# Gate and up projections of a SwiGLU block: eight block products per pair of weight tiles, or seven by Strassen's scheme

## The reference, cut to what matters

```
x = x + W_out( sigmoid(gA) * windowed_attention(h) + sigmoid(gB) * gated_linear_attention(h) )   # h = rmsnorm(x)
h = rmsnorm(x, g_ffn)
x = x + (silu(h @ w_gate) * (h @ w_up)) @ w_down        # w_gate, w_up: 1024 x 2816, w_down: 2816 x 1024
```

## Time and profile before

| | us |
|---|---|
| median of 3 runs | 994.57 |
| lowest and highest run | 994.55, 995.9 |
| span of the profiled execution | 994.7 |
| TensorE busy in it | 959.4 (96%) |
| DVE, ACT, POOL busy | 469.1, 352.6, 325.3 |

### The profile page before, as it was taken

The page is one execution under the profiler, slowest core; times in us unless marked ns, Lnnn a source line. Parts: engine busy times, 40 slices in busy tenths (PEclk is TensorE's granted clock), DMA queues, the critical chain, the costliest instruction groups (busy, mean ns, idle before and its releaser), DMA issues.

```text
span 994.7 us, 17842 instructions
## 1 busy us (share of the span) xinstructions
PE 959.4 (96%) x7171; PEld 897.7 (90%) x7171; DVE 469.1 (47%) x970; ACT 352.6 (35%) x661; POOL 325.3 (33%) x139
## 2 busy tenths in 40 slices
PE   3999999999889999999999999999999999999997
PEld 3899999988878787878789999999999999999997
DVE  5673656647777557776755344222113222122321
ACT  5542433434444444344434443222112222122231
POOL 2442312122222112222323334443334444334450
PEclk9999999999999999999999999999999999999999
DMA  8332213231222211121115222223223223323212
GB/s 228 88 84 64 75 53 65 53 75 51 69 65 64 64 43 43 52 56 43 43 29 168 86 85 86 84 84 105 86 80 89 84 84 91 91 77 90 65 55 68
DMA packets 148787, 76.34 MB, mean 77 GB/s; under 512 B 19280, under 2 KB 147622, under 8 KB 148726
## 3 DMA queue, kind: packets, MB, share of 16 engines
q1 hardware_dynamic: 142582, 71.88, 25.9%
q10 hardware_dynamic: 6144, 3.61, 1.3%
HBM read 71.87 MB, written 3.60 MB: 76 GB/s over the span
## 4 chain that ended last, share of the span: by engine, by line
PE 82%; DVE 12%; ACT 3%; issue 2%; DMA 1%; SPq 0%; ACTq 0%; DVEq 0%
PE G L487 23%; PE G L489 22%; PE G L488 22%; PE X L650 3%; PE X L621 2%; DVE qAT L1315 2%; PE X L634 2%; DVE den L1354 1%; DVE rs L1118 1%; DVE rs L1117 1%; DVE rt L1119 1%; DVE rv L1280 1%; DMA xtok<-in_x_sample_dram 1%; PE X L580 1%; ACT rs L894 1%
## 5 line engine op out<-in xcount | busy, mean ns | idle before, releaser
L465 POOL TENSOR_TENSOR w_lo<-wraw,w_hi 128x1024 fp32r<-128x1024 f32 x129 | 323.6, 2508 | 645.3 <-ACT w_hi L807 645.2
L487 PE MATMUL G<-h_hi,w_hi 128*128 128x272 f32 x1280 | 382.7, 299 | 11.0 <-DVE rv L1280 8.6
L489 PE MATMUL G<-h_hi,w_lo 128*128 128x272 f32 x1280 | 371.0, 290 | 0.0
L488 PE MATMUL G<-h_lo,w_hi 128*128 128x272 f32 x1280 | 369.0, 288 | 0.0
L487 PEld LDWEIGHTS G<-h_hi,w_hi 128*128 128x128 f32 x1280 | 241.6, 189 | 30.7 <-issue 28.0
L488 PEld LDWEIGHTS G<-h_lo,w_hi 128*128 128x128 f32 x1280 | 242.0, 189 | 0.6
L489 PEld LDWEIGHTS G<-h_hi,w_lo 128*128 128x128 f32 x1280 | 241.5, 189 | 0.0
L487 PE MATMUL G<-f_hi,w_hi 128*128 128x272 f32 x704 | 203.0, 288 | 0.0
L489 PE MATMUL G<-f_hi,w_lo 128*128 128x272 f32 x704 | 202.9, 288 | 0.0
L488 PE MATMUL G<-f_lo,w_hi 128*128 128x272 f32 x704 | 202.1, 287 | 0.0
L807 ACT ACTIVATE w_hi<-wraw 128x1024 fp32r<-128x1024 f32 x129 | 135.3, 1049 | 89.1 <-PE G L489 89.1
(11 more groups left out here) (217 smaller groups left out, 968.7 us busy)
## 6 DMA issues: line engine op xcount, KB each, us to landing
wraw<-in_w_in_dram SPq DMA_DIRECT2D x45, 512.0 KB
wraw<-in_w_gate_dram SPq DMA_DIRECT2D x22, 512.0 KB
wraw<-in_w_up_dram SPq DMA_DIRECT2D x22, 512.0 KB
wraw<-in_w_down_dram SPq DMA_DIRECT2D x16, 512.0 KB
xtok<-in_x_prompt_dram SPq DMA_DIRECT2D x8, 512.0 KB, 5.2
wraw<-in_w_in_dram SPq DMA_DIRECT2D x16, 256.0 KB
wraw<-in_w_out_dram SPq DMA_DIRECT2D x8, 512.0 KB
wraw<-in_w_down_dram SPq DMA_DIRECT2D x8, 384.0 KB
```

Of the source, the lines that this page charges most:

```text
L465: pool.tensor_tensor(w_lo[:, slot, :, :], wraw[:, slot, :, :], w_hi[:, slot, :, :].bitcast(F32), ALU.subtract).then_inc(w_split, 1)
L487: pe.matmul(o, w_hi[:, slot, kc, :], b_hi[:, kc, cols], start=(kc == 0), stop=False)
L488: pe.matmul(o, w_hi[:, slot, kc, :], b_lo[:, kc, cols], start=False, stop=False)
L489: mm = pe.matmul(o, w_lo[:, slot, kc, :], b_hi[:, kc, cols], start=False, stop=(kc == last))
```

## The change

For one pair of tiles, gate (n) and up (n+1), the weights are taken as a 2 x 2 matrix of blocks: A11 and A12 are the gate tile's first and last 512 input rows, A21 and A22 the up tile's. The activations are B11, B12 (first 512 features, frame halves one and two), B21, B22. Plain multiplication takes eight block products A x B of 4 chunks each; Strassen's scheme in Winograd's form takes seven with sums of blocks:

- DVE makes of the weights A21 + A22, A21 - A11 (in place in `wraw`), A21 + A22 - A11 and A12 - (A21 + A22 - A11) (`sums`); ACT rounds three of them to `c_hi` (`sums_high_part`), POOL subtracts for two low parts and DVE for one (`sums_low_part` on each).
- DVE makes of the activations B12 - B11 (`fa`) and, for the blocks 4 to 7, five kinds of input (`fb`), once, in the output projection (`ffn_input`).
- TensorE runs seven products of 12 matmuls per pair q (`gate_up`) into four banks, BANKS[q % 2]; three of them add onto a bank that ACT or DVE has read in between (`copy_p1`, `evict_early`). DVE puts the results together (`evict_early`, `evict_late`), and the silu follows one pair later (`gated`).
- The loops of the stage are written out instead of hardware loops. The residual comes by columns into a ring of two (`xcol`) instead of as whole rows, EARLY is 2 instead of 3, and the memory plan is another.

```diff
+PAIRS = [(g, GU0[g] + 2 * i) for g, m in enumerate(FF_GROUPS) for i in range(m)]
+FIRST = [sum(FF_GROUPS[:g]) for g in range(len(FF_GROUPS))]
...
-EARLY = 3
+EARLY = 2
...
+        BANKS = [[G[1][:, 0:TH], G[1][:, 512:512 + TH], G[0][:, 0:TH], G[0][:, 512:512 + TH]],
+                 [X[0][:, 0:TH], X[0][:, 512:512 + TH], X[1][:, 0:TH], X[1][:, 512:512 + TH]]]
...
+            def weights(n, w, row0, kc, col):
+                sp.wait_ge(w_split, n - RING + 1)
+                if n - RING in PAIR_OF:
+                    sp.wait_ge(sums_ok, PAIR_OF[n - RING] + 1)
...
+            def residual(i):
+                if i >= 2:
+                    sp.wait_ge(xt_done, i - 1)
+                c = slice(i * P, (i + 1) * P)
...
+                pool.wait_ge(c_hi_ok, 2 * q + 1)
+                pool.tensor_tensor(c_lo[q % 2][:, 0:2], csum[:, 0:2], c_hi[q % 2][:, 0:2].bitcast(F32),
+                                   ALU.subtract).then_inc(c_lo_ok, 1)
+            for n in range(N_TILES):
                 pool.wait_ge(hi_done, n + 1)
                 low_part(n % RING)
+                if n in PAIR_OF and n - 1 in PAIR_OF and PAIR_OF[n] == PAIR_OF[n - 1]:
+                    sums_low_part(PAIR_OF[n])
...
+            def product(bank, a_hi, a_lo, b_hi, b_lo, adds=False, ready=None):
+                for kc in range(HK):
+                    if ready is not None:
+                        pe.wait_ge(f_ok, ready + kc + 1)
+                    pe.matmul(bank, a_hi[:, kc, :], b_hi[:, kc, :], start=(kc == 0 and not adds), stop=False,
+                              skip_group_check=adds)
+                    pe.matmul(bank, a_hi[:, kc, :], b_lo[:, kc, :], start=False, stop=False, skip_group_check=adds)
+                    mm = pe.matmul(bank, a_lo[:, kc, :], b_hi[:, kc, :], start=False,
+                                   stop=(kc == HK - 1), skip_group_check=adds)
+                mm.then_inc(prod_done, 1)
...
+            def gate_up(q):
+                g, n = PAIRS[q]
+                s, r0, r1 = q % 2, n % RING, (n + 1) % RING
+                b1, b5, b6, b7 = BANKS[s]
+                k1, k2 = slice(0, HK), slice(HK, KC)
+                now = (lambda kc0: kc0) if q == 0 else (lambda kc0: None)
+                if q >= 2:
+                    pe.wait_ge(evicted, 6 * (q - 1))
+                if q == 1:
+                    pe.wait_ge(norm_done, len(NORMS) + 1)
+                if q == FIRST[g] and g == 0:
+                    pe.wait_ge(set_free[1], uses_before(n))
+                elif q == FIRST[g]:
+                    for r in range(2):
+                        pe.wait_ge(set_free[(n + r) % 2], uses_before(n + r))
+                product(b1, w_hi[:, r0, k1], w_lo[:, r0, k1], fa_hi[:, :, 0], fa_lo[:, :, 0],
+                        ready=now(0))
+                pe.wait_ge(c_lo_ok, q + 1)
+                product(b5, c_hi[s][:, 0], c_lo[s][:, 0], fa_hi[:, :, 1], fa_lo[:, :, 1])
+                if q == 0:
+                    pe.wait_ge(set_free[0], uses_before(n + 1))
+                product(b6, c_hi[s][:, 1], c_lo[s][:, 1], fb_hi[:, :, 3], fb_lo[:, :, 3], ready=now(HK))
+                if q == 0:
+                    x2_squares()
+                pe.wait_ge(w_split, n + 2)
+                product(b7, w_hi[:, r1, k1], w_lo[:, r1, k1], fb_hi[:, :, 2], fb_lo[:, :, 2])
+                pe.wait_ge(p1_ok, q + 1)
+                product(b1, w_hi[:, r0, k2], w_lo[:, r0, k2], fb_hi[:, :, 0], fb_lo[:, :, 0], adds=True)
+                pe.wait_ge(evicted, 6 * q + 2)
+                product(b7, w_hi[:, r1, k2], w_lo[:, r1, k2], fb_hi[:, :, 4], fb_lo[:, :, 4], adds=True)
+                pe.wait_ge(evicted, 6 * q + 3)
+                pe.wait_ge(c_lo4_ok, q + 1)
+                product(b5, c_hi[s][:, 2], c_lo[s][:, 2], fb_hi[:, :, 1], fb_lo[:, :, 1], adds=True)
...
+                if n in PAIR_OF and PAIRS[PAIR_OF[n]][1] != n:
+                    act.wait_ge(sums_ok, PAIR_OF[n] + 1)
+                act.activation(w_hi[:, n % RING, :, :], wraw[:, n % RING, :, :], ACT.Copy).then_inc(hi_done, 1)
...
+                act.wait_ge(fin_ok, i + 1)
+                dst, src = (fa_hi[:, i], fin[:, 0:2]) if i < HK else (fb_hi[:, i - HK], fin[:, :])
+                act.activation(dst, src, ACT.Copy).then_inc(f_hi_ok, 1)
                 if i >= 2:
                     act.wait_ge(x2_sum, i - 1)
                 act.activation(sq[:, i % 2, :], x2T[:, i, :], ACT.Square).then_inc(x2_sq, 1)
-                act.activation(f_hi[:, i, :], x2g[:, i % 2, :], ACT.Copy).then_inc(f_hi_ok, 1)
-                high_part(n + RING)
+                if n + RING < GU0[0] + 2:
+                    high_part(n + RING)
+                if i == KC - 2:
+                    sums_high_part(0, 0)
+                    sums_high_part(0, 1)
...
+                for q in range(FIRST[g], FIRST[g] + m):
+                    more = q + 1 < FIRST[g] + m
+                    first = PAIRS[q + 1][1] if more else DN0[g]
+                    copy_p1(q) if q == 0 else None
+                    high_part(first)
+                    if q > FIRST[g]:
+                        gate_tanh(q - 1)
+                    copy_p1(q) if q > 0 else None
+                    high_part(first + 1)
+                    if more:
+                        sums_high_part(q + 1, 0)
+                    if q > FIRST[g]:
+                        mid_high_part(q - 1)
+                    if more:
+                        sums_high_part(q + 1, 1)
+                gate_tanh(FIRST[g] + m - 1)
+                mid_high_part(FIRST[g] + m - 1)
...
+            def ffn_input(c):
+                gain = lambda i: param[:, G_FFN + i:G_FFN + i + 1]
+                raw_ab = fin[:, 0:2, :].rearrange("p a n -> p (a n)")
+                link(dve.tensor_scalar(raw_ab, x2T[:, c, :], gain(c), None, ALU.mult))
+                if c < HK:
+                    dve.tensor_tensor(fin[:, 1, :], fin[:, 1, :], fin[:, 0, :], ALU.subtract).then_inc(fin_ok, 1)
+                    return
+                was = x2T[:, c - HK, :]
+                link(dve.scalar_tensor_tensor(out=fin[:, 2, :], in0=was[:, TH:T], scalar=gain(c - HK),
+                                              in1=fin[:, 1, :], op0=ALU.mult, op1=ALU.subtract))
+                link(dve.scalar_tensor_tensor(out=fin[:, 3, :], in0=was[:, 0:TH], scalar=gain(c - HK),
+                                              in1=fin[:, 2, :], op0=ALU.mult, op1=ALU.subtract))
+                dve.tensor_tensor(fin[:, 4, :], fin[:, 0, :], fin[:, 3, :], ALU.subtract).then_inc(fin_ok, 1)
...
+            def sums(q):
+                _, n = PAIRS[q]
+                r0, r1 = n % RING, (n + 1) % RING
+                dve.wait_ge(wload[r0], 32 * (n // RING + 1))
+                dve.wait_ge(wload[r1], 32 * ((n + 1) // RING + 1))
+                if q >= 1:
+                    dve.wait_ge(c_lo_ok, q)
+                    dve.wait_ge(c_lo4_ok, q)
+                a11, a12 = wraw[:, r0, 0:HK], wraw[:, r0, HK:KC]
+                a21, a22 = wraw[:, r1, 0:HK], wraw[:, r1, HK:KC]
+                link(dve.tensor_tensor(csum[:, 0], a21, a22, ALU.add))
+                dve.tensor_tensor(a21, a21, a11, ALU.subtract)
+                link(dve.tensor_tensor(csum[:, 1], csum[:, 0], a11, ALU.subtract))
+                dve.tensor_tensor(csum[:, 2], a12, csum[:, 1], ALU.subtract).then_inc(sums_ok, 1)
+            def sums_low_part(q):
+                dve.wait_ge(c_hi_ok, 2 * q + 2)
+                dve.tensor_tensor(c_lo[q % 2][:, 2], csum[:, 2], c_hi[q % 2][:, 2].bitcast(F32), ALU.subtract)\
+                    .then_inc(c_lo4_ok, 1)
+            def evict_early(q):
+                b1, b5, b6, b7 = BANKS[q % 2]
+                dve.wait_ge(prod_done, 7 * q + 3)
+                dve.wait_ge(p1_ok, q + 1)
+                dve.tensor_tensor(u2[:, :], b6, p1[:, :], ALU.add).then_inc(evicted, 1)
+                dve.wait_ge(evicted, 6 * q + 1)
+                dve.wait_ge(prod_done, 7 * q + 4)
+                dve.tensor_tensor(u3[:, :], b7, u2[:, :], ALU.add).then_inc(evicted, 1)
+                dve.wait_ge(evicted, 6 * q + 2)
+                dve.tensor_tensor(up[:, TH:T], b5, u3[:, :], ALU.add).then_inc(evicted, 1)
+            def evict_late(q):
+                b1, b5, b6, b7 = BANKS[q % 2]
+                dve.wait_ge(prod_done, 7 * q + 5)
+                dve.tensor_tensor(sg[:, 0:TH], b1, rt[:, 0:TH], ALU.mult).then_inc(evicted, 1)
+                dve.wait_ge(prod_done, 7 * q + 6)
+                dve.tensor_tensor(up[:, 0:TH], b7, u2[:, :], ALU.add).then_inc(evicted, 1)
+                dve.wait_ge(prod_done, 7 * q + 7)
+                dve.tensor_tensor(sg[:, TH:T], b5, u2[:, :], ALU.add).then_inc(evicted, 1)
+                dve.wait_ge(evicted, 6 * q + 6)
+                dve.tensor_tensor(sg[:, TH:T], sg[:, TH:T], rt[:, TH:T], ALU.mult).then_inc(gate_ok, 1)
+            def gated(q):
+                dve.wait_ge(silu_ok, q + 1)
```

(112 more changed lines are left out.)

266 lines of the change are left out of this document (93 added, 173 removed).

## The result

| | before | after |
|---|---|---|
| median of 4 runs, us (lowest to highest) | 994.63 (994.55 to 995.9) | **1074.88** (1072.74 to 1077.31) |
| ratio (95% interval) | 1 | 1.0805 (1.0785 to 1.0825) |
| profiled execution: span | 994.7 | 1071.6 (time 1073.28, mean granted clock 0.965) |

The change costs 8% in time, though TensorE has 264 matmuls fewer. The forecast was 1059, its range 1016 to 1090.

A forecast was written before the change was run, and what follows sets the result against it. TensorE bound the kernel before; afterwards DVE and POOL, excluding each other, would make it wait. Terms 41.3 + 18.2 + 2.9 + 1.8 + 0.6 = +64.8 on 994.7 us gave about 1059 us, range 1016 to 1090.

The forecast's parts named there:

- 16 middle pairs: Gate/up pairs neither first nor last in a group: each takes 14.9 us instead of 12.03.
- start of the stage with group 0's first pair: Output tiles to end of first pair: late sums and inputs cost +18.2 us, less 1.5 for its missing product.
- first pairs of groups 1 and 2, G banks: These pairs take 10.5 us, 1.5 less each; waiting for both G banks after the last down tile adds 1.8.
- last pair of a group: Without sums but with two blocks of 2.4 us on DVE, this pair takes 12.05 us.
- starts of the down projections: The time saved by fewer products no longer covers TensorE's lead-in to the down projections; +2.9 us in all.
- input side (EARLY), all else: EARLY 2 puts a third ACT copy before the gate behind a 0.5 us wait after the input tiles: +0.6 us.
- Exclusion and its size: DVE operations with two SBUF inputs and POOL subtractions exclude each other; together they need 12.6 us a middle pair.
- the last paragraph: Signs listed: blocked operations at 2 to 3 us, TensorE idle 4 us before product six, pairs near 15 us.
- rival 1: No exclusion for these DVE operations; TensorE stays the bound at 10.53 us a pair, 975 us total; chance 0.08.
- hand schedule: A middle pair laid out by hand on all engines: TensorE waits 4.3 us for DVE, period 14.9 us.
- rival 4: TensorE runs two products slowly after each wait: 2.4 us more a pair, up to +38, 1097 us; chance 0.07.
- ACT's wait for the first sums: At the stage's start, this wait on ACT makes the add of output tile 6 come 5 us late.

The follow-up runs named there:

- Experiment 1: Against the kernel after, POOL's three subtractions per pair became memsets that read nothing; 989.31 us, ratio 0.994 to the kernel before.
- experiment 3: Against the kernel after, 26 unused matmuls fill TensorE's wait before product six in 16 middle pairs; 1052.54 us, ratio 1.057 to the kernel before.
- Experiment 7: Against the kernel after, ACT rounds pair 0's up tile after its copies for output tile 6; 1071.0 us, ratio 1.075 to the kernel before.

## Why the prediction was right, and where it was off

The direction, the mechanism and the range held; the median is 15.9 us (1.5%) above the forecast. By its terms, in the profiled span (+76.9 against +64.8):

| term | forecast | measured |
|---|---|---|
| 16 middle pairs | 16 x (14.9 - 12.03) = +45.9 | 247.3 - 192.5 = +54.8 |
| start of the stage with group 0's first pair | +18.2 - 1.5 | 43.4 of group 0 less 23.4 of its middle pairs = +20.0 |
| first pairs of groups 1 and 2, G banks | -3.0 + 1.8 | 31.2 of both groups less 31.4 of their middle pairs = -0.2 |
| last pair of a group | 12.05 | 12.0 |
| starts of the down projections | +2.9 | +2.4 |
| input side (EARLY), all else | +0.6 | -0.1 (that wait is 0.78 instead of 0.5) |

**Exclusion and its size: right.** Blocked operations at 2.2 to 2.8 us ending about 0.6 after POOL, those on PSUM untouched, TensorE waiting before product six for DVE: all as the last paragraph listed. Experiment 1 takes the exclusion away and gets rival 1's 10.53 us a pair.

**A middle pair: near by luck, two errors against each other.** At full clock it is 14.0, not 14.9. The hand schedule had TensorE's fifth product at 7.55 (it was 7.6 here) and u3 at 11.8 (it was 10.7): evict_late ended at about 0.9 instead of 1.45, so the sums ended 0.75 sooner and POOL's second subtraction began 0.9 sooner (706.16, which is 6.9 after the end of the pair before). TensorE's wait was forecast at 4.3 and is 3.1. The hand schedule overcounts the 16 middle pairs by 13.6 us (14.05 instead of 14.9 each); the clock, which it leaves out, adds 22.5 (247.3 less 16 x 14.05). The difference is the 8.9 in the first row of the table.

**The step that failed: rival 4, put aside at 0.07.** "If the two products behind each wait run at the slow pitch": in 12 of 16 middle pairs one of the two does (3.0 us instead of 1.5), which puts on 1.4, not 2.4; in two pairs both do, and in two neither. 14.0 + 1.4 is 15.4. The trace of before had only the pitch of 0.22 at the start of the run as a sign, and the forecast weighed a stage without pauses against it. The page that spoke for it (Trainium skill, TensorE: Matmul & The Clock Gate, section HAM oscillation) was right in 14 of the 16 pairs: the granted clock is 0.89 over pairs with a wait of 3.1, and 1.00 over those of experiment 3, where the wait is filled.

**The last pair of a group: right.** Two blocks of 2.5 and 2.8 us (716.36, 718.89) put u3 at 8.6 us, forecast 9.0.

**The start: right within 3.3 us.** The chain of waits came as named: c_lo 6.47 (594.24), the last input block 1.88 (601.25), the copy of P1 1.18, u3 4.52 (614.50). The forecast had 29.8 to the end of the first pair against 33.1; the products between the waits ran at a pitch of 0.226, which it didn't count. Experiment 7 shows one link of it mis-sized: ACT's wait for the first sums held the add of tile 6 for 2.5 us, not 5.

**Unsettled.** Why one middle pair in group 1 and one in group 2 (14.05 and 14.06, the second of each group's middle pairs) kept the clock: their wait was about as long (3.24 ahead of 813.56). The traces show that it is so, not why.

## What to carry to other kernels

A saving on TensorE is bought with elementwise work; before adding up busy times, sort the other engine's operations by whether they read two SBUF tiles, and count POOL's reading beside each of them as if both ran on one engine: that sum is a lower end. Then lay one period out by hand, and where TensorE would wait some 3 us in every period, as here, reckon with a slow clock behind it, in most periods if not in all. If the helper engine has room in every second period only, use the cheaper scheme in every second one: eight pairs of 22 won 1.2%, where all 22 lost 8%.
